# Rows of the last two experts under each other, returned in one product of 128 rows, with gating out of PSUM and the other picks on GpSimd

## What is computed

```
def moe(h, router_w, router_b, w_gate, w_up, w_down):
    ...
    gates = jnp.sum(jax.nn.one_hot(idx, N_EXPERTS, dtype=jnp.float32) * w[..., None], axis=1)
    a = jnp.einsum("td,edf->tef", h, w_gate)
    u = jnp.einsum("td,edf->tef", h, w_up)
    z = jax.nn.silu(a) * u * gates[:, :, None].astype(h.dtype)
    return jnp.einsum("tef,efd->td", z, w_down)
...
    h2 = rmsnorm(x, norm2_g) * (1 + scale2) + shift2
    x = x + gate2 * moe(h2.reshape(bsz * l, -1), router_w, router_b, w_gate, w_up, w_down).reshape(bsz, l, -1)
```

## Time and profile before

| | |
|---|---|
| median of 3 runs | 1264.37 us (1260.73 to 1267.17) |
| profiled execution, its own time | 1264.38 us |
| its span | 1262.5 us |
| mean granted TensorE clock | 0.936 of full |
| ends of the two layers' experts | about 617 us and 1233 us |

### The profile page before, as it was taken

How to read it: one execution, slowest core, us unless ns; L and a number is a source line. 1 busy time by engine, 2 the same in 40 slices (tenths; PEclk the granted TensorE clock), 3 DMA queues, 4 the chain that set the end, 5 groups by cost and what they waited for, 6 DMA issues and landing times.

```text
span 1262.5 us, 18212 instructions
## 1 busy us (share of the span) xinstructions
PE 1127.8 (89%) x6966; PEld 525.2 (42%) x6966; DVE 481.4 (38%) x1243; ACT 383.9 (30%) x704; POOL 234.6 (19%) x339
## 2 busy tenths in 40 slices
PE   3999989899899888888899999989998998888886
PEld 1555546454433223232354655546444332233332
DVE  1374776734532011110255756675245111111106
ACT  2223444431332212221322334453233322222213
POOL 1231384220011111100200226441101011110100
PEclk9999999889899989998889997997998998999996
DMA  9839631764898999999830313066624899999982
GB/s 365 301 138 178 108 107 67 282 241 173 353 334 341 391 408 399 403 406 399 319 123 17 125 67 100 11 250 221 266 102 173 348 347 407 398 392 400 401 336 102
DMA packets 51213, 325.08 MB, mean 257 GB/s; under 512 B 6710, under 2 KB 7126, under 8 KB 32576
## 3 DMA queue, kind: packets, MB, share of 16 engines
q1 hardware_dynamic: 39296, 293.16, 59.5%
q0 software_dynamic: 10560, 26.17, 8.5%
q10 hardware_dynamic: 1280, 4.72, 0.9%
HBM read 316.15 MB, written 22.25 MB: 268 GB/s over the span
## 4 chain that ended last, share of the span: by engine, by line
PE 61%; DMA 24%; DVE 10%; issue 3%; ACT 1%; SPq 1%; DVEq 0%; ACTq 0%; POOLq 0%
DMA ring<-moe_w_up 19%; PE ps L2094 18%; PE ps L1727 13%; PE ps L1783 7%; PE ps L1984 7%; PE ps L1743 3%; PE ps L2205 3%; DVE attT L1285 2%; PE ps L1766 2%; DMA ring<-ada_w 2%; PE ps L1878 2%; PE ps L1907 1%; PE ps L1733 1%; PE ps L2083 1%; DMA expert_rows<-big,lst 1%
## 5 line engine op out<-in xcount | busy, mean ns | idle before, releaser
L2094 PE MATMUL ps<-ring,dbuf 128*32 128x512 f32 x2336 | 364.2, 609 | 30.8 <-DMA ring<-moe_w_up 22.6
L2094 PE MATMUL ps<-extra,dbuf 128*32 128x512 f32 x1408 | 222.8, 624 | 31.3 <-DMA ring<-moe_w_up 23.5
L2094 PEld LDWEIGHTS ps<-ring,dbuf 128*32 128x32 f32 x2336 | 100.8, 112 | 201.6 <-issue 191.8
L1727 PE MATMUL ps<-ring,extra 128*128 128x512 f32 (+1 forms) x384 | 149.9, 550 | 0.0
L1571 DVE COPY dbuf<-ps 128x256 f32<-128x256 f32 (+1 forms) x32 | 15.4, 483 | 284.3 <-PE ps L2083 284.3
L2094 PEld LDWEIGHTS ps<-extra,dbuf 128*32 128x32 f32 x1408 | 64.9, 114 | 133.9 <-issue 133.7
L1783 PE MATMUL ps<-extra,ring 128*128 128x384 f32 x320 | 107.3, 494 | 0.0
L840 POOL DMA_INDIRECT expert_rows<-big,lst x28 | 26.3, 940 | 421.8 <-ACT big L1117 223.4
L1727 PEld LDWEIGHTS ps<-ring,extra 128*128 128x128 f32 x384 | 74.0, 194 | 69.8 <-issue 66.2
L1984 PE MATMUL ps<-ring,extra 128*128 128x512 f32 x192 | 84.3, 594 | 3.1 <-DVE extra L1460 1.8
L1783 PEld LDWEIGHTS ps<-extra,ring 128*128 128x128 f32 x320 | 60.9, 193 | 41.3 <-issue 2.5
(11 more groups left out here) (298 smaller groups left out, 1423.8 us busy)
## 6 DMA issues: line engine op xcount, KB each, us to landing
ring<-moe_w_up SPq DMA_DIRECT2D x30, 2048.0 KB, 21.4
ring<-ada_w SPq DMA_DIRECT2D x24, 2048.0 KB, 8.8
ring<-moe_w_down SPq DMA_DIRECT2D x20, 2048.0 KB, 21.7
extra<-moe_w_gate SPq DMA_DIRECT2D x18, 2048.0 KB, 18.0
ring<-moe_w_gate SPq DMA_DIRECT2D x14, 2048.0 KB, 20.5
ring<-w_in SPq DMA_DIRECT2D x12, 2048.0 KB, 20.0
extra<-moe_w_down SPq DMA_DIRECT2D x12, 2048.0 KB, 24.6
ring<-w_out SPq DMA_DIRECT2D x4, 2048.0 KB, 8.2
```

What stands on the lines that cost most here:

```text
L1727: ins = pe.matmul(out, a, b, start=(n == 0), stop=(n == len(pairs) - 1))
L2094: return pe.matmul(p[QT * g:QT * (g + 1), :], a, w, start=start, stop=stop, tile_position=(0, QT * g))
```

## The change

- Expert 14's result goes from PSUM to rows 0 to 63 of `ybuf[:, s]` and expert 15's to rows 64 to 127, for each token group s once: DVE multiplies by `gate[:, s]` on the way (`gated_rows`). ACT no longer copies these two results.
- `late` becomes one matrix of 128 rows for each tile, and each tile and half takes one product of 128 rows.
- The sum of the other picks is gated and added to `x` apart from these: by POOL for tiles 0 and 1, by DVE for tile 2 (`added`). `completed(t)` adds the banks straight to `x`, after POOL is done with the tile.
- The turn of expert 15's products stands in the middle of expert 14's product with the down weights; DVE copies expert 14's turned products and ACT expert 15's, into a place of its own. Expert 15's result goes to the bank of "dn1".
- The three normalisations stand together at the end.

```
@@ POOL, behind the last scatter of a layer, ahead of final_norm_g
+                for t in range(NT - 1):
+                    y = yr[0][:, t, :]
+                    pool.wait_ge(s_sum, NT * l + t + 1)
+                    step(pool.tensor_tensor(y, y, gate[:, min(t, 1), :], ALU.mult))
+                    pool.tensor_tensor(x[:, t, :], x[:, t, :], y, ALU.add).then_inc(s_px, 1)
@@ ACT, expert()
-                    if not first:
+                    if not first and (last or next_):
                         p, cap = ready(act, ("zt", l), e - 1), cap_of(i, es - 1)
...
-                    if last:
-                        act.wait_ge(s_late, l + 1)
-                        first_picks(0)
-                        first_picks(1)
...
-                    if not first:
+                    if not first and next_:
                         p = ready(act, ("dn0", l), e - 1)
...
                     if last:
-                        first_picks(2)
                         act.activation(rneg[:, 0, :], eps, ACT.Sqrt)
+                        act.wait_ge(s_late, l + 1)
+                        for t in range(NT):
+                            first_picks(t)
@@ DVE
+                def gated_rows(j):
+
+                    job, n = (("dn0", l), NE - 2) if j == 0 else (("dnz", l), 0)
+                    p, r = ready(dve, job, n), slice(SMALL * j, SMALL * (j + 1))
+                    for s in range(2):
+                        for b in range(2):
+                            h = slice(SMALL * b, SMALL * (b + 1))
+                            c = slice(512 * b, 512 * (b + 1))
+                            if j == 0 and b == 0:
+                                dve.wait_ge(d_sc[s], 16 * ((NE - LATE) // 2) * (l + 1))
+                            ins = dve.tensor_tensor(late_rows(s)[r, c], p[h], gate[h, s, c], ALU.mult)
+                            if 2 * s + b == 3:
+                                release(dve, ins, job, n)
+                            elif j == 0:
+                                step(ins)
+                            else:
+                                ins.then_inc(s_fold, 1)
+
+                def added(t):
+
                     y = yr[0][:, t, :]
                     step(dve.tensor_tensor(y, y, gate[:, min(t, 1), :], ALU.mult))
-                    dve.tensor_tensor(x[:, t, :], x[:, t, :], y, ALU.add).then_inc(s_x, 1)
+                    step(dve.tensor_tensor(x[:, t, :], x[:, t, :], y, ALU.add))
+
+                def completed(t):
+
+                    if t < NT - 1:
+                        dve.wait_ge(s_px, (NT - 1) * l + t + 1)
+                    for b in range(2):
+                        job, xs = ("cm", l, t, b), x[:, t, b * 512:(b + 1) * 512]
+                        p = ready(dve, job)
+                        release(dve, dve.tensor_tensor(xs, xs, p, ALU.add), job)
+                    dve.engine_nop().then_inc(s_x, 1)
                     dve.wait_ge(s_x, NT * (2 * l + 1) + t + 1)
...
+                gated_rows(0)
                 summed(0)
+                gated_rows(1)
                 summed(1)
-                expert(NBODY, 0, last=True, next_=False)
+                completed(0)
                 summed(2)
-                completed(0)
+                added(2)
                 completed(1)
-                normalize(2 * l + 2, 0)
                 completed(2)
-                normalize(2 * l + 2, 1)
-                normalize(2 * l + 2, 2)
+                for t in range(NT):
+                    normalize(2 * l + 2, t)
@@ PE
                         for f in range(FC):
+                            if f == FC // 2 and not last and not next_:
+                                turn_products(es)
                             for g in range(4):
...
-                moved(pe, ("dn0", l), NE - 2)
                 for t in range(NT):
                     for b in range(2):
-                        begin(pe, ("cm", l, t, b))
-                    returned(t, 0)
-                    if t == 0:
-                        moved(pe, ("dn0", l), NE - 1)
-                    returned(t, 1)
+                        job, s = ("cm", l, t, b), min(t, 1)
+                        p = begin(pe, job)
+                        if t == 0 or (t, b) == (1, 0):
+                            pe.wait_ge(s_fold, 3 * l + 2 * s + b + 1)
+                        if (t, b) == (1, 1):
+                            moved(pe, ("dnz", l))
+                        fill(pe.matmul(p, late[:, t, :], late_rows(s)[:, b * 512:(b + 1) * 512], start=True, stop=True), job)
```

More of the change, by code:

```diff
@@ L209, in place_jobs @@
             place[(kind, l)] = (b, uses[b] + 1)
-            uses[b] += uses_before(kind, NE)
+            uses[b] += uses_before(kind, NE) - (kind == "dn0")
+        b = EJOBS.index("dn1")
+        uses[b] += 1
+        place[("dnz", l)] = (b, uses[b])
         for n_cm, kind in enumerate(("xt0", "xt1", "a", "u", "zt", "dn0")):
@@ L309, in hybrid_step @@
         yr = [carve(buf, 0, NT, D) for buf in (big, bbuf)]
-        late = carve(bbuf, NT * D, LATE, NT, P)
+        late = carve(bbuf, NT * D, NT, P)
         fin = ring[:, SLOTS - 1, 0:D]
@@ L522, in block_read @@
                 kind, e = queued(blk[2])
-                kind = read_by(kind, e)
-                ready(sp, (kind, blk[1]), uses_before(kind, e))
+                if (kind, e) == ("dn1", NE - 1):
+                    ready(sp, ("dnz", blk[1]))
+                else:
+                    kind = read_by(kind, e)
+                    ready(sp, (kind, blk[1]), uses_before(kind, e))
             else:
@@ L1096, in expert @@
                             act.activation(by_chunk(sS)[0:SMALL], in_rows(p)[SMALL:P], ACT.Silu).then_inc(s_silu, 1)
[L1097 removed]
+                    if not first and (last or next_):
                         p, cap = ready(act, ("zt", l), e - 1), cap_of(i, es - 1)
[L1099 to L1103 removed]
+                        release(act, act.activation(last_products if last else products_turned(cap), turned_rows(p, cap), ACT.Copy), ("zt", l), e - 1)
                     if next_:
@@ L1571, in turned_out, with expert @@
                     release(dve, dve.tensor_copy(rows_turned(at, cap)[:, 0:4, :], turned_rows(p, cap)), ("xt0", l), e)
-                def expert(i, es, first=False, last=False, next_=True):
+                def expert(i, es, first=False, next_=True):
                     e = i * EXP_PER_BODY + es
@@ L1577, in expert @@
                         turned_out(e + 1, (es + 1) % 2, cap_of(i, es + 1))
-                    if not last and cap_of(i, es) == SMALL:
+                    else:
+                        p, cap = ready(dve, ("zt", l), e - 1), cap_of(i, es - 1)
+                        release(dve, dve.tensor_copy(products_turned(cap), turned_rows(p, cap)), ("zt", l), e - 1)
+                    if cap_of(i, es) == SMALL:
                         p = ready(dve, ("a", l), e)
@@ L1584, in expert @@
                                                               op0=ALU.mult, op1=ALU.mult), ("a", l), e)
-                    elif not last:
+                    else:
                         n_u = use_of("u", i, es)
@@ L1669, in _ @@
                 dve.tensor_scalar(kept, kept, -1.0, 1.0, ALU.mult, ALU.add).then_inc(s_late, 1)
[L1670 to L1673, removed]
+                for j in range(LATE):
+                    for t in range(NT):
+                        apart(dve.tensor_scalar(tokf[SMALL * j:SMALL * (j + 1), t:t + 1], lst[0:SMALL, NE - LATE + j, 0:1],
+                                                -float(P * t), None, ALU.add))
+                settled()
+                step(dve.tensor_tensor(late, places.unsqueeze(1).broadcast_to([P, NT, P]), tokf.unsqueeze(2).broadcast_to([P, NT, P]),
+                                       ALU.is_equal))
                 for e in range(EXP_PER_BODY):
@@ L1682, in summed @@
                     y = yr[0][:, t, :]
[L1683 to L1691, removed]
+                    dve.scalar_tensor_tensor(out=y, in0=yr[1][:, t, :], scalar=kept[:, NT + t:NT + t + 1], in1=y, op0=ALU.mult,
+                                             op1=ALU.add).then_inc(s_sum, 1)
@@ L2124, in expert, with turn_products @@
                         fill(ins, ("a", l), e)
-                    if not first:
-                        moved(pe, *product_of(l, i, es - 1))
-                        turn("zt", e - 1, [zb[0:CAP, f * P:(f + 1) * P] for f in range(FC)])
+                    def turn_products(es):
+                        moved(pe, *product_of(l, i, es))
+                        turn("zt", i * EXP_PER_BODY + es, [zb[0:CAP, f * P:(f + 1) * P] for f in range(FC)])
+                    if not first and not last:
+                        turn_products(es - 1)
                     if next_:
```

23 lines of the change are left out of this document (12 added, 11 removed).

## The result

Median of 17 runs each: 1255.83 us (1249.34 to 1262.98) with the change, 1263.64 (1257.09 to 1271.23) without. The ratio is 0.9939, 95% interval 0.9918 to 0.9960: faster, by 7.8 us. The forecast was 1256.8 us, 7.6 faster. The profiled execution took 1254.32 us, its span 1252.6.

What follows compares the result with a forecast made beforehand. The last-ending chain was 61% PE; at layer ends it ran over PE's slow-clock products, then DVE's normalisations. Gains of 5.4 (first layer) and 2.2 us (second) sum to 7.6, giving 1256.8 us; range 1247.5 to 1263.

Steps and rivals of the forecast that it cites:

- PE leaves the path: Layer ends: returned products in 12 records take 5.2 us (high clock) or 10.4 (low), ending before DVE's completions.
- DVE and POOL: Layer ends: POOL's operations take 2.35 us each and hold DVE's two-SBUF-input operations; first layer's normalisations end 639.25, before 644.55.
- the sum: Whole kernel: DVE and POOL taking turns at each layer's end, 5.4 + 2.2 = 7.6 us gained, 1256.8 us.
- The row of 2.14 us: Earlier trace: a 0.17 us DVE operation took 2.14 beside POOL, cited as evidence that POOL holds DVE.
- Free overlap: Rival, both layer ends: POOL and DVE work side by side unhindered, 16.5 us gained, 1247.9 us; chance 0.15.
- The clock's price: First layer's end: PE idles waiting for DVE, then restarts at the low clock, costing 2.4 us.
- First layer: End of the first layer: transposes begin in effect at 641.8 in place of 647.16, 5.4 us gained.
- Last layer: End of the second layer: last normalisation ends at 1257.2 in place of 1259.4, 2.2 us gained.
- The gain of the final norm: Second layer: its load, issued about 1245.3, lands 4.3 us later at no cost; rival 9.9 us, costing 3.8, chance 0.10.
- the row of x_prompt: Earlier trace: a 512 KB load on ACT's queue took 4.3 us, used to price the final gain's load.
- The moved turn: Last experts' products on PE: removes most of two copy waits, but worth nothing as DVE waits for tile 0's sum.

Runs made afterwards that it cites:

- e0: The changed kernel run again with no edit: median 1259.23 us, ratio 0.9948 to the kernel before.
- e2: Changed kernel with each returned product of 128 rows replaced by two of 64 rows, on PE alone: 1266.76 us, ratio 1.0019 to the kernel before.
- e11: The changed kernel a third time, no edit, on another chip: median 1258.14 us, ratio 0.9961 to the kernel before.
- e4: Changed kernel with the turn of expert 15's products put back behind expert 14's down product: 1256.70 us, ratio 0.9952 to the kernel before.
- e5: Kernel before, with ACT copying the last expert's result out of PSUM ahead of gating tile 1's first picks: 1263.03 us, ratio 0.9999.
- e1: Changed kernel with POOL's gates and residuals of tiles 0 and 1 given back to DVE: 1263.94 us, ratio 0.9999 to the kernel before.
- e8: Changed kernel with all gates and residuals on DVE, a second run on another chip: 1264.24 us, ratio 0.9997 to the kernel before.
- e6: Changed kernel with POOL keeping only the gates of tiles 0 and 1 and DVE doing the additions: 1256.11 us, ratio 0.9925 to the kernel before.
- e3: Changed kernel with 18 filler products in place of 9 behind the first layer's returned products: 1256.46 us, ratio 0.9913 to the kernel before.

## Why the prediction was right

*PE leaves the path*: shown. The products took 5.39 us (forecast 5.2 at the high clock; 7.08 in e0, still inside the 10.4 that the forecast allowed), the filler ended 8.47 us before the transposes, and with 64 rows PE is back on the path in the first layer (e2).

*DVE and POOL*: shown, and to a tenth. POOL's operation was forecast at 2.35 and took 2.35; the second sum beside it, where it did not wait for a load, was forecast at 3.2 (619.7 to 622.9) and took 3.02. From the first sum the sum gave 23.69 us to the last normalised tile (615.56 to 639.25) and the trace has 23.68; in the last layer 25.2 (1232.04 to 1257.2) against 24.93. The rule of the Trainium skill (SBUF — State Buffer, "SBUF: two separate sides") agrees in both directions: the sum at 625.15 ends 1.07 us behind POOL's gate, and POOL's residual at 626.12 ends 2.20 behind that sum. The row of 2.14 us that I leaned on was weaker support than I made it: a one-input operation on two columns. The scans of the same rows, which do have two inputs in SBUF, say it better: 0.39 with no arithmetic of POOL beside them (702.17), up to 1.42 with it (89.26). Free overlap, 1247.9, is refuted by the rows of the changed kernel.

*The clock's price*: 2.4 forecast, 4.85 - 2.78 = 2.1 measured here, 1.5 in e0.

*First layer*: 5.4 forecast; the first product of the projection came 5.0 us earlier (644.78 against 649.78), though the turn before it came 1.3 later, so 6.3 in M. *Last layer*: 2.2 forecast, 2.4 in A, 3.75 in M; the other 1.3 are loads of the picks that were issued earlier against the turn, which I had counted at nothing, and which e11 does not have.

*The gain of the final norm* landed 4.0 us after its issue (the page's part 6), 2.4 ahead of its reader: the row of x_prompt (4.3) was the right one.

```profile
ring<-final_norm_g POOLq DMA_DIRECT2D x1, 512.0 KB, 4.0
```

*The moved turn* was worth nothing (e4), as forecast.

What the sum did not have is that the 17.31 us of the earlier trace rows need not be a constant of the kernel before: e5 and the last layer of e2 show such products at the high clock. Against the one trace the two stretches gained 6.3 and 3.75 us by M, 10.0 where I had 7.6, and they are the whole difference of the profiled spans (9.9 us, 1262.5 to 1252.6). Over many executions the gain is smaller, 7.8, 7.4 and 6.2 us in the medians. That it met my 7.6 so closely is in part luck: I had argued from one execution with the low clock in both layers, and had left small gains at nothing, and the two errors went opposite ways.

The sum also fails for the kernels that leave one part out. By it e1 and e8, with DVE alone, should have kept most of the gain, and they kept none (0.9999, 0.9997). e2, with POOL but without the fold, kept none either (1.0019, M first at 43.48 as before the change). So each of the two parts alone is worth nothing that these medians can tell (intervals of some 0.3% to either side), and together they are worth 6 to 8 us. That is measured; by what road, the clock's part included, is not settled.

## What to carry to other kernels

Give POOL elementwise work where DVE reads PSUM at that moment (e6: 2.35 us hidden whole); beside DVE operations with two SBUF inputs the two take turns, and each must be priced at the wait. When a change takes PE off the path, ask at which clock it comes back: nine cheap products in the idle time were worth 1.7 us of the stretch and 2.8 of the median (e3). Measure a difference below 1% over many executions on the same chip: the way to the first stretch alone differed by 6.2 us between executions of the changed kernel (607.45 to 613.61), about what the change is worth.

## What the runs showed of the hardware

Products of 64 rows ran mostly at a granted clock of 0.50 in the kernel before and in the first layer of e2 (for over 20 us of a busy PE, with the 128-row filler behind them also low, 10.74 us for 18 records in place of 7.89), and at 1.00 in the last layer of e2 and in e5. Products of 128 rows met 0.50 too, for some 3 us in e0 (7.08 us in place of 5.39).

The execution's mean granted clock goes with its time: 0.924 to 0.955 over 89 executions of the kernel before, correlation -0.87, 6.5 us for each 0.01. Two arrangements of the same work that differ by 1.1 to 2.0 us of DVE's time differed by 6.1 us in the median and 0.0055 in the clock.
